# A seven-product down projection of 64-token blocks, with all token transposes between its first and second stretch

## The chip, the cores and the metric

One core of one Trainium2 chip runs the whole program. The metric is the device time of one execution in microseconds (us), median over the runs shown. TensorE (PE) multiplies, VectorE (DVE) and ScalarE (ACT) work element by element, GpSimd (POOL) issues the indirect transfers, SyncE (SP) issues the plain ones. Everything is float32.

## What is computed

A decoder block: a mixer (short convolution and a recurrent part), then a mixture of 32 experts of which each token takes 4, then a norm. The part that matters here is one expert's block of tokens:

```
h = xb @ gu_w[e] + gu_b[e]
x_glu = jnp.minimum(h[:, 0::2], SWIGLU_LIMIT)
x_lin = jnp.clip(h[:, 1::2], -SWIGLU_LIMIT, SWIGLU_LIMIT)
act = x_glu * jax.nn.sigmoid(SWIGLU_ALPHA * x_glu) * (x_lin + 1.0)
return act @ dn_w[e] + dn_b[e]
```

`gu_w[e]` is 1024 x 2048, `dn_w[e]` is 1024 x 1024. The result is scaled by the token's gate and added to the token's row of the output sum.

## The kernel before

The program first computes the mixer and the router (about a third of the time), and then goes through the 32 experts one after the other. An expert has room for 160 tokens: 128 in a full tile and 32 in "the rest". The rest's output is folded, four pieces of 32 tokens by 256 columns stacked on 128 partitions (`Y2`).

All engines run their own loop over the experts and meet at semaphores. TensorE's loop (`expert_pe`) is one turn behind itself: turn `n+1` first finishes expert `n` and then starts the next one. In a turn stand, in this order:

- `down_half(n, 0)`, L2083: 8 products of the activations (128 tokens as stationary operand, 128 rows of the feed-forward dimension each) with 512 columns of the down weights, into bank 2 of PSUM;
- `transpose_tokens`, L2102 and L2108: the gathered token rows of the expert after next (`xg`, and `xg2` for the rest) are transposed through the identity into banks 4, 5 and 7, from which ScalarE copies them into `xT` (`copy_xT`, L992 and L995);
- `down_rest(n)`, L2093, if the expert has more than 128 tokens: 32 products in tiles of 32 columns of the array, four side by side, into bank 6; otherwise one tiny product in its place (L2126);
- `down_half(n, 1)`, L2083 again: the other 512 columns, into bank 3;
- `gate_up`, L2063 (and its last 6 products, L2072): 128 products for the next expert, 16 for each of the 8 steps f, alternating between banks 0 and 1. The moving operand has 128, 144 or 160 tokens, by the size of the expert.

Every float32 product is two matmul records in the trace. VectorE follows with `glu`: for each f two additions and clips out of PSUM (L1468, L1469), then after ScalarE's sigmoid (L1000) two more operations (L1472, L1475) into `actT`. Step f of `gate_up` waits (`s_gd`) until the L1468 and L1469 of step f-2 have read their bank. At the end of the expert VectorE adds the bias to each finished bank (L1485 the first half, L1487 the rest, L1489 the second half), ScalarE scales by the gate (L1011, L1013, L1015), and GpSimd scatters the rows into the sum in memory (L703, L705). GpSimd's queue has, in this order: read the next list of tokens (L672, L673), gather those tokens (L687, L689), read the list for the scatter, scatter. The gather can start only when its list has landed, and that list is read behind the scatter of the expert before.

SyncE loads the weights: six slots of 2 MB, four for gate and up (`gu_w`), two for down (`dn_w`). The down slots of an expert are loaded when the down products of the expert before are done, that is when `gate_up` of the same expert starts.

Of the kernel before, what the change touches and what calls it, by code (L numbers as in the profile page):

```python
# [13 lines left out]
P = 128  # L14
# [101 lines left out]
def build(nc, x, xT_d, w_in_t, prm_d, lora_d, wgate_d, normw_d, w_out, router_w, router_b, gub_d, gu_w, dn_w,  # L116
          dn_b, consts_d, list0_d, entry_d, out, conv_d, bonus_d, xn_d, acc_d, list_d):
    ctx = ExitStack()
    with ctx:
# [121 lines left out]
        wslot = [at(o, KT, HALF) for o in (0, 16, 32, 64, 80, 96)]  # L241
        xg = at(48, D)
# [16 lines left out]
        sums = [at(112 + 8 * g, GROUP, D) if g < 3 else at(56, GROUP, D) for g in range(GROUPS)]  # L259
# [35 lines left out]
        s_ccp = sem("cc_copied")  # L295
        s_u = sem("u_made")
# [45 lines left out]
        s_wt = [sem(f"expert_w{u}") for u in range(6)]  # L342
# [4 lines left out]
        s_dn, s_db, s_yr, s_ye, s_l1 = sem("dn"), sem("dn_bias_in"), sem("y_rows"), sem("dn_read"), sem("lin")  # L347
        s_md = sem("experts_done")
# [51 lines left out]
        def weights_of(e, u):  # L400

            src = gu_w[bass.ds(4 * e + u, 1)] if u < 4 else dn_w[bass.ds(2 * e + u - 4, 1)]
            return src.rearrange("a p k n -> (a p) k n")
# [25 lines left out]
        def _(sp):  # L429
# [121 lines left out]
            for u in (2, 3, 4, 5):  # L551
                sp.dma_start(wslot[u], weights_of(0, u)).then_inc(s_wt[u], 16)

            def expert_weights(lo, r):
                with sp.Fori(lo, E) as e:
                    for u in range(6):

                        n = r * E + e
                        if u < 4:
                            sp.wait_ge(s_gu, 8 * n + 2 * u - 6)  # L560
                        else:
                            sp.wait_ge(s_dn, 3 * n)
                        sp.dma_start(wslot[u], weights_of(e, u)).then_inc(s_wt[u], 16)
                    sp.wait_ge(s_ye, 3 * n + 6)
                    bias_in(e)

            def sums_in():
                for g in range(GROUPS):
                    lo, hi = g * GROUP, (g + 1) * GROUP
                    sp.dma_start(sums[g], acc_d[lo * P:hi * P, :].rearrange("(t p) n -> p t n", p=P)).then_inc(s_x[g], 16)  # L570
# [4 lines left out]
            def experts_sp(r):  # L575
# [5 lines left out]
                sums_in()  # L581
# [21 lines left out]
        def _(pool):  # L603
# [6 lines left out]
            for ahead, by in ((s_ye, 6), (s_xe, 3), (s_gd, KT), (s_act, KT)):  # L610
                pool.sem_inc(ahead, by)
# [157 lines left out]
        def _(act):  # L769
# [232 lines left out]
            def expert_act(r):  # L1002
                copy_xT(r * (E + 1))
                with act.Fori(0, E - 1 if isinstance(r, int) else E) as e:
# [5 lines left out]
                    act.wait_ge(s_ye, 3 * n + 7)  # L1010
                    nc.scalar.activation(Yt[:, 0:HALF], Yt[:, 0:HALF], ACT.Copy, scale=gate).then_inc(s_yr, 1)  # L1011
                    act.wait_ge(s_ye, 3 * n + 8)
                    nc.scalar.activation(Y2, Y2, ACT.Copy, scale=gate2).then_inc(s_yr, 1)  # L1013
                    act.wait_ge(s_ye, 3 * n + 9)
                    nc.scalar.activation(Yt[:, HALF:D], Yt[:, HALF:D], ACT.Copy, scale=gate).then_inc(s_yr, 1)  # L1015
# [8 lines left out]
            def last_expert_act():  # L1024
# [14 lines left out]
                act.wait_ge(s_ye, 3 * n + 7)  # L1039
                nc.scalar.activation(sqj3[:, 0:HALF], rows[:, 0:HALF], ACT.Square, accum_out=rows_sq[:, 0:1]).then_inc(s_sq2, 1)  # L1040
                act.wait_ge(s_ye, 3 * n + 8)
                act.wait_ge(s_sq2, 2 * TT + 1)
                nc.scalar.activation(sqj3[:, 0:PW], rows2, ACT.Square, accum_out=rows_sq[:, 2:3]).then_inc(s_sq2, 1)
                act.wait_ge(s_ye, 3 * n + 9)
# [20 lines left out]
        def _(dve):  # L1065
# [202 lines left out]
            for h in range(2):  # L1268
                dve.wait_ge(s_ccp, h + 1)
                dve.wait_ge(s_pcv, 2 + h + 1)  # L1270
                nc.vector.tensor_tensor(u_cv[:, 2 + h * HALF:2 + (h + 1) * HALF], ccs[:, h * HALF:(h + 1) * HALF],
                                        ps[:, ring_pair(NR + 1) + h, :], ALU.mult).then_inc(s_u, 1)
            dve.wait_ge(s_u, 2)
# [202 lines left out]

            def expert_dve(r):
                with dve.Fori(0, E - 1 if isinstance(r, int) else E) as e:
                    n = r * E + e
                    for f in range(KT):  # L1480
                        glu(n, e, f)
                    dve.wait_ge(s_scr, n + 1)
                    dve.wait_ge(s_db, 16 * (PIECES + 1) * (n + 1))
                    dve.wait_ge(s_dn, 3 * n + 1)
                    nc.vector.tensor_tensor(Yt[:, 0:HALF], ps[:, 2, :], dnb[:, 0:HALF], ALU.add).then_inc(s_ye, 1)  # L1485
                    dve.wait_ge(s_dn, 3 * n + 2)
# [719 lines left out]
```

## Time and profile before

| | |
|---|---|
| runs shown | 2274.15, 2276.58, 2279.27 us; median 2276.58 us |
| profiled execution | 2280.95 us, of which the span from first to last instruction is 2279.3 us |
| TensorE busy | 2226.0 us, 98% of the span |
| VectorE, ScalarE, GpSimd busy | 781.6, 473.7, 343.5 us (34%, 21%, 15%) |
| DMA queues | 55.2% and 7.8% of 16 engines' span |
| mean granted clock of TensorE | 0.99 |

Busy shares are means over stages with different limits. A matmul record overlaps the next one, so the time that a product takes from TensorE is the distance between starts of records and not the duration of one.

### The profile page before, as it was taken

The numbers are of one execution on the slowest core, as the hardware profiler recorded it, in microseconds if no ns is written. First come the engines' busy times: TensorE is split into PE (matmuls) and PEld (weight loads), VectorE is DVE, ScalarE is ACT, GpSimd is POOL, SyncE is SP. The second block draws the span as 40 slices with busy tenths as digits, with TensorE's granted clock in tenths as the row PEclk, the third lists the DMA queues.
The fourth block names the chain that finished last, engine by engine and source line by source line (L and its number), as shares of the span: only waits on it lengthen the run. The fifth ranks groups of instructions, "written<-read, shape, count | busy, mean of one in ns | idle before, by whom it ended". The sixth has DMA issues, their size and how long they took to land.

```text
span 2279.3 us, 46156 instructions
## 1 busy us (share of the span) xinstructions
PE 2226.0 (98%) x18230; PEld 1644.5 (72%) x18231; DVE 781.6 (34%) x1853; ACT 473.7 (21%) x988; POOL 343.5 (15%) x360
## 2 busy tenths in 40 slices
PE   8999998899999999999999999999999999999997
PEld 3444445888445778887788878788778887788875
DVE  6465543455434222222222222232222232223224
ACT  3232001444333111111211111111111111111113
POOL 0000001121022212111121211122111121121112
PEclk9999999999998999999999999999999999999998
DMA  3111112334433767977777977789777988678877
GB/s 142 60 50 46 55 55 63 96 104 132 174 138 103 310 253 298 332 307 300 293 301 291 350 300 269 260 335 348 300 276 277 333 348 308 253 295 331 347 295 260
DMA packets 111411, 534.99 MB, mean 235 GB/s; under 512 B 26771, under 2 KB 60711, under 8 KB 86752
## 3 DMA queue, kind: packets, MB, share of 16 engines
q1 hardware_dynamic: 89200, 489.30, 55.2%
q0 software_dynamic: 22160, 44.98, 7.8%
q8 instruction: 36, 0.59, 0.1%
q14 instruction: 15, 0.12, 0.0%
HBM read 485.24 MB, written 40.05 MB: 230 GB/s over the span
## 4 chain that ended last, share of the span: by engine, by line
PE 95%; DMA 2%; DVE 1%; issue 1%; POOL 0%; ACT 0%; SPq 0%; POOLq 0%; DVEq 0%
PE ps L2063 39%; PE ps L2083 19%; PE ps L1571 9%; PE ps L1669 5%; PE ps L1942 5%; PE ps L2093 2%; PE ps L2072 2%; PE ps L1768 2%; PE ps L1618 1%; PE ps L1777 1%; PE ps L2102 1%; PE ps L1750 1%; DMA idx_g<-list_s 1%; PE ps L1782 1%; PE ps L1870 1%
## 5 line engine op out<-in xcount | busy, mean ns | idle before, releaser
L2063 PEld LDWEIGHTS ps<-arena 128*128 128x128 f32 x7808 | 925.9, 191 | 16.6 <-issue 15.1
L2063 PE MATMUL ps<-arena 128*128 128x128 f32 (+2 forms) x7808 | 926.9, 281 | 1.3 <-ACT arena L995 1.3
L2083 PE MATMUL ps<-arena 128*128 128x512 f32 x1024 | 454.3, 596 | 0.0
L2083 PEld LDWEIGHTS ps<-arena 128*128 128x128 f32 x1024 | 190.7, 190 | 221.8 <-issue 221.1
L1468 DVE TENSOR_SCALAR arena<-ps,arena 128x160 f32<-128x160 f32 x256 | 98.2, 384 | 620.1 <-PE ps L2063 536.1
L1000 ACT ACTIVATE arena<-arena 128x160 f32<-128x160 f32 x256 | 86.1, 336 | 828.3 <-DVE arena L1468 828.3
L1571 PE MATMUL ps<-arena 128*128 128x512 f32 x448 | 195.7, 594 | 0.0
L703 POOL DMA_INDIRECT sum_s<-arena,idx_s x31 | 51.5, 1663 | 824.6 <-ACT arena L1015 824.6
L1571 PEld LDWEIGHTS ps<-arena 128*128 128x128 f32 x448 | 84.5, 190 | 109.4 <-issue 109.4
L1669 PE MATMUL ps<-arena 128*128 128x512 f32 x280 | 120.6, 592 | 0.8 <-ACT arena L844 0.8
L1942 PE MATMUL ps<-arena 128*128 128x512 f32 x256 | 113.7, 594 | 0.0
L1669 PEld LDWEIGHTS ps<-arena 128*128 128x128 f32 x280 | 53.1, 190 | 68.1 <-issue 67.8
L1472 DVE SCALAR_TENSOR_TENSOR arena<-arena 128x160 f32<-128x160 f32 x256 | 83.3, 325 | 49.9 <-ACT arena L1000 48.9
L1469 DVE TENSOR_SCALAR arena<-ps,arena 128x160 f32<-128x160 f32 x256 | 95.9, 375 | 0.0
L687 POOL DMA_INDIRECT arena<-xn_s,idx_g x33 | 36.6, 1109 | 390.7 <-DMA idx_g<-list_s 361.4
L1489 DVE TENSOR_TENSOR arena<-ps,arena 128x512 f32<-128x512 f32 x31 | 21.4, 692 | 205.4 <-PE ps L2083 205.4
L1942 PEld LDWEIGHTS ps<-arena 128*128 128x128 f32 x256 | 47.6, 190 | 55.2 <-issue 54.9
L1475 DVE TENSOR_TENSOR arena<-arena 128x160 f32<-128x160 f32 x256 | 83.1, 325 | 8.8
L992 ACT COPY arena<-ps 128x512 f32<-128x512 f32 x66 | 35.4, 588 | 209.2 <-PE ps L2102 209.2
L1485 DVE TENSOR_TENSOR arena<-ps,arena 128x512 f32<-128x512 f32 x31 | 21.4, 691 | 158.6 <-PE ps L2083 158.6
L1015 ACT ACTIVATE arena<-arena,idx_s 128x512 f32<-128x512 f32 x31 | 22.4, 722 | 202.1 <-DVE arena L1489 202.1
L1768 PE MATMUL ps<-arena 64*64 64x64 f32 x1328 | 56.8, 224 | 6.2 <-issue 3.8
(271 smaller groups left out, 1965.5 us busy)
## 6 DMA issues: line engine op xcount, KB each, us to landing
arena<-gu_w SPq DMA_DIRECT2D x128, 2048.0 KB, 11.7
arena<-dn_w SPq DMA_DIRECT2D x64, 2048.0 KB, 14.6
arena<-dn_b SPq DMA_DIRECT2D x32, 512.0 KB, 16.2
arena<-w_in_t SPq DMA_DIRECT2D x26, 512.0 KB, 3.2
arena<-arena SPq DMA_DIRECT2D x50, 256.0 KB, 2.7
arena<-w_out SPq DMA_DIRECT2D x2, 2048.0 KB, 8.4
arena<-x SPq DMA_DIRECT2D x8, 512.0 KB, 5.2
xn_s<-arena SPq DMA_DIRECT2D x8, 512.0 KB, 2.7
```

The source lines that it names most:

```text
L703: pool.indirect_dma_start(acc_d, bass.IndirectOffsetOnAxis(ap=idx_s[:, 0:1], axis=0), Yt, None, compute_op=ALU.add).then_inc(s_sc, 16)
L1000: nc.scalar.activation(sgm[f % 2], gt[f % 2], ACT.Sigmoid, scale=ALPHA).then_inc(s_gs, 1)
L1468: nc.vector.tensor_scalar(gt[b], ps[:, b, 0:C], g0, LIMIT, ALU.add, ALU.min).then_inc(s_g1, 1)
L1469: nc.vector.tensor_scalar(lt[b], ps[:, b, C:2 * C], g1, LIMIT + 1, ALU.add, ALU.min).then_inc(s_gd, 1)
L1472: nc.vector.scalar_tensor_tensor(out=lt[b], in0=lt[b], scalar=1 - LIMIT, in1=sgm[b], op0=ALU.max, op1=ALU.mult).then_inc(s_l1, 1)
L1475: nc.vector.tensor_tensor(actT[:, f, :], lt[b], gt[b], ALU.mult).then_inc(s_act, 1)
L1571: last = nc.tensor.matmul(ps[:, bank + h, :], win[:, slot, kt * P:(kt + 1) * P], xnT[:, kt, h * HALF:(h + 1) * HALF], start=kt == 0, stop= ...
L1669: last = nc.tensor.matmul(ps[:, bank, :], weights[:, k * P:(k + 1) * P], tokens[:, k, :], start=start and k == 0, stop=stop and k == K2 - ...
L1768: last = nc.tensor.matmul(out_at(s, 0, h if l == 0 else 1 - h, r), MTs[s][own(h), r, :], Tst[s][own(h), r, :], start=True, stop=True)
L1942: last = nc.tensor.matmul(ps[:, 2 * (t % 2) + h, :], (mix_conv, mix_y)[part][:, k, t * P:(t + 1) * P], (woA, woB)[part][:, k, h * HALF:(h ...
L2063: last = nc.tensor.matmul(ps[:, f % 2, k * C:k * C + size], wslot[u][:, kt, o:o + P], xT[:, kt, 0:size], start=kt == 0, stop=kt == KT - 1, ...
L2083: last = nc.tensor.matmul(ps[:, 2 + h, :], actT[:, ft, 0:P], wslot[4 + h][:, ft, :], start=ft == 0, stop=ft == KT - 1)
```

## The change

The 128-token part of the down projection is split in four 64-token by 512-row blocks of activations and four 512-row by 512-column blocks of weights (d11, d12, d21, d22), and computed with seven products of blocks in place of eight, by sums and differences of blocks (Winograd's form of Strassen's scheme). One block product is 4 float32 matmuls with a stationary operand of 64 tokens. Two block products run side by side on the lower and upper 64 columns of the array (`both`). The seventh is cut in two halves of 256 columns that run side by side. The last expert keeps the old form, outside of the loop.

VectorE makes four sums of weight blocks (128 x 2048 elements each, in two pieces of 128 x 1024) between the `glu` steps, five small sums of activation blocks, and takes the results together in more and partly smaller steps than before. The down weights come in four transfers of 1 MB. The transposes stand between the first and the second stretch of products.

```diff
-            def down_rest(n):
+            def both(low, high, done):
+
+                for k in range(K2):
+                    for rows, (bank, acts, weights, first) in ((lower, low), (upper, high)):
+                        width = weights.shape[-1]
+                        last = nc.tensor.matmul(ps[rows, bank, 0:width], acts[:, k, :], weights[:, k, :],
+                                                start=first and k == 0, stop=k == K2 - 1, skip_group_check=True)
+                if done:
+                    last.then_inc(s_dn, 1)
+            def down_first(n, q, o):
+                pe.wait_ge(s_wd1, 32 * n + 32)
+                pe.wait_ge(s_as, 5 * q + 5 + 1)
+                pe.wait_ge(s_ds, 8 * q + 8 + 4)
+                pe.wait_ge(s_ye, o + 5)
+                both((2, a11, d11, True), (3, a_low, d12, True), True)
+            def down_second(n, q, o):
+                pe.wait_ge(s_as, 5 * q + 5 + 3)
+                pe.wait_ge(s_ds, 8 * q + 8 + 6)
+                pe.wait_ge(s_wd21, 16 * n + 16)
+                pe.wait_ge(s_ye, o + 6)
+                both((2, a_dif, d_mix, False), (2, a12, d21, True), True)
+            def down_third(n, m, q, o):
+                pe.wait_ge(s_ds, 8 * q + 8 + 8)
+                pe.wait_ge(s_xe, 3 * m + 4)
+                pe.wait_ge(s_ye, o + 7)
+                both((2, a_sum, d_dif, False), (4, a22, d_all, True), True)
+                pe.wait_ge(s_as, 5 * q + 5 + 5)
+                pe.wait_ge(s_ye, o + 8)
+                both((6, a_all, d22[:, :, 0:PW], True), (6, a_all, d22[:, :, PW:HALF], True), True)
...
                     with pe.If(turn > 0):
-                        down_half(n, 0)
+                        down_first(n, q, o)
                     size = size_at(turn)
-                    transpose_tokens(m)
+                    transpose_tokens(m, 0)
+                    transpose_tokens(m, 1)
+                    with pe.If(turn > 0):
+                        down_second(n, q, o)
                     with pe.If(size > 1):
-                        down_rest(n)
+                        down_rest(n, o, q)
...
                     with pe.If(turn > 0):
-                        down_half(n, 1)
+                        down_third(n, m, q, o)
```

```diff
+            def down_sums(n, q, f):
+                if f == 2:
+                    dve.wait_ge(s_wd1, 32 * n + 32)
+                    for h in range(2):
+                        down_sum(d_dif, d12, d11, ALU.subtract, h)
+                if f in (3, 4):
+                    dve.wait_ge(s_wd22, 16 * n + 16)
+                    down_sum(d12, d12, d22, ALU.subtract, f - 3)
+                if f in (4, 5):
+                    dve.wait_ge(s_ds, 8 * q + 8 + f - 3)
+                    down_sum(d_mix, d22, d_dif, ALU.subtract, f - 4)
+                if f == 6:
+                    dve.wait_ge(s_wd21, 16 * n + 16)
+                    for h in range(2):
+                        dve.wait_ge(s_ds, 8 * q + 8 + 5 + h)
+                        down_sum(d_all, d21, d_mix, ALU.subtract, h)
...
                     for f in range(KT):
                         glu(n, e, f)
+                        down_sums(n, q, f)
+                        if f == K2:
+                            dve.wait_ge(s_act, 8 * n + KT + K2)
+                            act_sum(q, a_low, a21, a11, ALU.subtract, 0)
+                    dve.wait_ge(s_act, 8 * n + KT + KT)
+                    act_sum(q, a_sum, a21, a22, ALU.add, 1)
+                    act_sum(q, a_dif, a_sum, a11, ALU.subtract, 2)
...
+                    dve.wait_ge(s_dn, o + 1)
+                    nc.vector.tensor_tensor(y_first[upper], ps[lower, 2, :], dnb[lower, 0:HALF], ALU.add).then_inc(s_ye, 1)
...
+                    dve.wait_ge(s_dn, o + 2)
+                    nc.vector.tensor_tensor(Yt[upper, 0:HALF], ps[lower, 2, :], dnb[lower, 0:HALF], ALU.add).then_inc(s_ye, 1)
+                    dve.wait_ge(s_ye, o + 7)
+                    nc.vector.tensor_tensor(Yt[lower, 0:HALF], y_first[upper], ps[upper, 2, :], ALU.add)
+                    nc.vector.tensor_tensor(Yt[upper, 0:HALF], Yt[upper, 0:HALF], ps[upper, 3, :], ALU.add).then_inc(s_yp, 1)
```

On TensorE, a turn of the loop in the kernel before stood so, from the first half of the down projection (bank 2) over the transposes and the rest (or the tiny product in its place) to the second half:

```order
L2083 MATMUL ps<-arena 128x512 [waits act_ready]
L2083 MATMUL ps<-arena 128x512 x6
...
L2102 MATMUL ps<-cst,arena 128x128 [waits tokens_gathered]
L2102 MATMUL ps<-cst,arena 128x128 x7
L2108 MATMUL ps<-cst,arena 128x128 [waits pieces_gathered]
...
L2093 MATMUL ps<-arena 32x256 [waits dn_read]
L2093 MATMUL ps<-arena 32x256 x31
...
L2083 MATMUL ps<-arena 128x512 [waits dn_read]
L2083 MATMUL ps<-arena 128x512 x7
```

In the changed kernel the same stretch stands so (L2199 is the line in `both`; 64 is the width of the stationary operand):

```order
L2199 MATMUL ps<-arena 64x512 [waits dn_read]
L2199 MATMUL ps<-arena 64x512 x7
...
L2234 MATMUL ps<-cst,arena 128x128 [waits tokens_gathered]
L2240 MATMUL ps<-cst,arena 128x128 [waits pieces_gathered]
...
L2199 MATMUL ps<-arena 64x512 [waits dn_read]
L2199 MATMUL ps<-arena 64x512 x7
...
L2182 MATMUL ps<-arena 32x256 [waits dn_read]
...
L2199 MATMUL ps<-arena 64x512 [waits dn_read]
L2199 MATMUL ps<-arena 64x512 x7
...
L2199 MATMUL ps<-arena 64x256 [waits dn_read]
L2199 MATMUL ps<-arena 64x256 x7
```

Two stretches of eight full-width products became three of eight half-width ones and one of eight that are half as wide and half as long; the transposes now come after the first of four stretches, and each stretch waits for a read by VectorE.

On VectorE, the end of an expert in the kernel before, from the last operation of the last `glu`:

```order
L1475 TENSOR_TENSOR arena<-arena 128x160 [waits lin]
L1482 REGISTER_ALU
L1483 REGISTER_ALU [waits expert_rows_free]
L1484 ISA [waits dn_bias_in]
L1485 TENSOR_TENSOR arena<-ps,arena 128x512 [waits dn]
L1486 REGISTER_ALU
L1487 TENSOR_TENSOR arena<-ps,arena 128x256 [waits dn]
L1488 REGISTER_ALU
L1489 TENSOR_TENSOR arena<-ps,arena 128x512 [waits dn]
```

And in the changed kernel, from the sums after the last `glu` to the last reads of PSUM:

```order
L1549 TENSOR_TENSOR arena<-ps,arena 64x512 [waits dn]
...
L1554 TENSOR_TENSOR arena<-ps,arena 64x512 [waits dn]
L1556 TENSOR_TENSOR arena<-arena,ps 64x512 [waits dn_read]
L1557 TENSOR_TENSOR arena<-arena,ps 64x512
...
L1559 TENSOR_TENSOR arena<-ps,arena 128x256 [waits dn]
...
L1561 TENSOR_TENSOR arena<-ps,arena 64x512 [waits dn]
L1562 TENSOR_TENSOR arena<-ps,arena 64x256
...
L1565 TENSOR_TENSOR arena<-arena,ps 64x512 [waits third_quarter_steps]
...
L1567 TENSOR_TENSOR arena<-arena,ps 64x512 [waits third_quarter_steps]
...
L1569 TENSOR_TENSOR arena<-arena,ps 64x256 [waits dn]
L1571 TENSOR_TENSOR arena<-arena,ps 64x256
```

Three reads of PSUM became eleven.

Two smaller parts: at the end of the program the sums are read back into the first two weight slots, and SyncE waits for the last expert's first steps before it issues those reads; and two semaphores of the convolution became one, whose first waiter now waits for both copies.

## Rows read from the trace of the kernel before

**Rows 1.** The page: the chain that ended last, share of the span by engine

```profile
PE 95%; DMA 2%; DVE 1%; issue 1%; POOL 0%; ACT 0%; SPq 0%; POOLq 0%; DVEq 0%
```

**Rows 2.** Timeline of TensorE, down part with rest: start us, us, engine, line, count

```profile
1974.88 7.03 PE L2083 MATMUL ps<-arena 128*128 128x512 f32 x16
1981.75 1.04 PE L2102 MATMUL ps<-cst,arena 128*128 128x128 f32 x8
1982.93 3.66 PE L2093 MATMUL ps<-arena 128*32 128x256 f32 x64
1986.52 7.13 PE L2083 MATMUL ps<-arena 128*128 128x512 f32 x16
1993.49 30.05 PE L2063 MATMUL ps<-arena 128*128 128x144 f32 x244
```

**Rows 3.** Timeline of TensorE, down part without rest

```profile
2072.51 7.03 PE L2083 MATMUL ps<-arena 128*128 128x512 f32 x16
2079.37 1.04 PE L2102 MATMUL ps<-cst,arena 128*128 128x128 f32 x8
2080.24 0.38 PE L2108 MATMUL ps<-cst,arena 128*128 128x128 f32 x2
2080.56 0.25 PE L2126 MATMUL ps<-cst,arena 128*32 128x32 f32 x2
2080.74 7.13 PE L2083 MATMUL ps<-arena 128*128 128x512 f32 x16
2087.71 27.41 PE L2063 MATMUL ps<-arena 128*128 128x128 f32 x244
```

**Rows 4.** Groups by line: all products of the rest

```profile
L2093 PE MATMUL ps<-arena 128*32 128x256 f32 x960 | 54.9, 380 | 0.0
```

**Rows 5.** Line L1875 in the recurrent part: durations ns, first and last start

```profile
L1875 PE MATMUL ps<-arena x16: 222/222/222, 411.1 to 411.5; 128*64 128x64 f32 x16
```

**Rows 6.** Timeline of VectorE in the turn of rows 3

```profile
2054.66 0.38 DVE L1468 TENSOR_SCALAR arena<-ps,arena 128x160 f32<-128x160 f32 x1 [2.04 <-PE ps L2063]
...
2068.95 0.38 DVE L1468 TENSOR_SCALAR arena<-ps,arena 128x160 f32<-128x160 f32 x1 [2.03 <-PE ps L2063]
...
2072.94 0.39 DVE L1468 TENSOR_SCALAR arena<-ps,arena 128x160 f32<-128x160 f32 x1 [2.45 <-PE ps L2072]
...
2074.16 0.33 DVE L1475 TENSOR_TENSOR arena<-arena 128x160 f32<-128x160 f32 x1
2079.57 0.69 DVE L1485 TENSOR_TENSOR arena<-ps,arena 128x512 f32<-128x512 f32 x1 [5.09 <-PE ps L2083]
```

**Rows 7.** Groups by line: VectorE on 1024 and on 256 elements

```profile
L1113 DVE TENSOR_TENSOR arena<-arena 128x1024 f32<-128x1024 f32 x14 | 17.1, 1224 | 44.9 <-ACT arena L791 44.9
L1487 DVE TENSOR_TENSOR arena<-ps,arena 128x256 f32<-128x256 f32 x31 | 13.2, 424 | 69.6 <-PE ps L2093 60.3 <-PE ps L2126 9.3
```

**Rows 8.** Down weights of one expert: SyncE's issue, and issue to landing

```profile
2088.05 0.89 SPq L563 DMA_DIRECT2D arena<-dn_w  x2
...
DMA to landing us min/median/max: 7.8/11.2/14.6
```

**Rows 9.** Timeline of GpSimd: the scatter behind the turn of rows 3

```profile
2090.22 1.67 POOL L703 DMA_INDIRECT sum_s<-arena,idx_s  x1 [23.20 <-ACT arena L1015]
```

**Rows 10.** DMA queues in 2051 to 2059.5 (two rows), then in 2072 to 2074.5 us

```profile
q1 hardware_dynamic: 215, 2.25, 64.9%
q0 software_dynamic: 210, 0.59, 35.9%
...
q0 software_dynamic: 55, 0.06, 6.6%
```

**Rows 11.** The chain that ended last, in order of time: the list behind the last scatter

```profile
2226.05 12.33 DMA idx_g<-list_s
```

**Rows 12.** Timeline of TensorE: the first time it reaches L2072

```profile
783.99 2.60 PE L2072 MATMUL ps<-arena 128*128 128x160 f32 x12 [2.94 <-issue]
```

**Rows 13.** Busy time by stretch: span, PE, PEld, DVE, ACT, POOL, clock, DMA share, GB/s

```profile
2043.60:2087.70 44.10, 44.10 (x301) 36.16 (x300) 12.41 (x35) 7.06 (x15) 8.10 (x8) 1.00 0.86 325
```

More of the change, by code:

```diff
@@ L241, in build @@
         wslot = [at(o, KT, HALF) for o in (0, 16, 32, 64, 80, 96)]
+        K2, TH = KT // 2, P // 2
+        d11, d21 = wslot[4][:, 0:K2, :], wslot[4][:, K2:KT, :]
+        d12, d22 = wslot[5][:, 0:K2, :], wslot[5][:, K2:KT, :]
+        d_dif, d_mix, d_all = (at(o, K2, HALF) for o in (112, 120, 128))
+        a_sum, a_dif, a_low, a_all = (at(56 + k, K2, TH) for k in range(4))
+        a_rest = at(60, K2, REST)
+        y_first, y_both = at(61, HALF), at(53, HALF)
         xg = at(48, D)
@@ L258, in build @@
         GROUPS = TT // GROUP
-        sums = [at(112 + 8 * g, GROUP, D) if g < 3 else at(56, GROUP, D) for g in range(GROUPS)]
+        sums = [at(8 * g, GROUP, D) for g in range(GROUPS)]
         rows, rows2 = at(178, D), at(182, PW)
@@ L341, in build @@
         s_mi = sem("moe_inputs")
-        s_wt = [sem(f"expert_w{u}") for u in range(6)]
+        s_wt = [sem(f"expert_w{u}") for u in range(4)]
+        s_wd1, s_wd22, s_wd21 = (sem(f"down_w{k}") for k in ("12_11", "22", "21"))
+        s_ds, s_as = sem("down_weight_sums"), sem("act_sums")
         s_ig, s_gx, s_is, s_sc = (sem("gather_list_in"), sem("tokens_gathered"), sem("scatter_list_in"),
@@ L609, in _ @@
                 pool.sem_inc(ahead, by)
-            for ahead, by in ((s_ye, 6), (s_xe, 3), (s_gd, KT), (s_act, KT)):
+            for ahead, by in ((s_ye, 5), (s_xe, 3), (s_gd, KT), (s_act, KT), (s_as, 5), (s_ds, 8)):
                 pool.sem_inc(ahead, by)
@@ L2076, in down_half @@
             def down_half(n, h):
-                pe.wait_ge(s_wt[4 + h], 16 * n + 16)
-                pe.wait_ge(s_ye, 3 * n + 4 + 2 * h)
+                pe.wait_ge(s_wd1, 32 * n + 32)
+                pe.wait_ge((s_wd21, s_wd22)[h], 16 * n + 16)
+                pe.wait_ge(s_ye, 5 * n + 5)
                 for ft in range(KT):
@@ L2085, in down_half, with down_rest @@
                 last.then_inc(s_dn, 1)
-            def down_rest(n):
-                pe.wait_ge(s_wt[5], 16 * n + 16)
-                pe.wait_ge(s_ye, 3 * n + 5)
+            def down_rest(n, o, q=None):
+                if q is not None:
+                    pe.wait_ge(s_as, 5 * q + 5 + 4)
+                pe.wait_ge(s_wd1, 32 * n + 32)
+                pe.wait_ge(s_wd22, 16 * n + 16)
+                pe.wait_ge(s_wd21, 16 * n + 16)
+                pe.wait_ge(s_ye, o + 5)
                 for ft in range(KT):
                     for g in range(PIECES):
-                        last = nc.tensor.matmul(ps[g * REST:(g + 1) * REST, 6, 0:PW], actT[:, ft, P:C],
+                        rows = a_rest[:, ft - K2, :] if q is not None and g >= 2 and ft >= K2 else actT[:, ft, P:C]
+                        last = nc.tensor.matmul(ps[g * REST:(g + 1) * REST, 6, 0:PW], rows,
                                                 wslot[4 + g // 2][:, ft, g % 2 * PW:(g % 2 + 1) * PW],
@@ L2096, in down_rest, with no_rest @@
                 last.then_inc(s_dn, 1)
-            def transpose_tokens(m):
-                pe.wait_ge(s_gx, 16 * m + 16)
-                for kt in range(KT):
+            def no_rest(o):
+                pe.wait_ge(s_ye, o + 5)
+                nc.tensor.matmul(ps[0:REST, 6, 0:REST], actT[:, 0, P:C], ident[:, 0:REST], start=True, stop=True
+                                 ).then_inc(s_dn, 1)
+            lower, upper = slice(0, TH), slice(TH, P)
+            def both(low, high, done):
[6 more added lines that the diff above has]
+                    last.then_inc(s_dn, 1)
@@ new lines, in down_third, with transpose_tokens @@
+            def down_third(n, m, q, o):
[6 more added lines that the diff above has]
+                both((6, a_all, d22[:, :, 0:PW], True), (6, a_all, d22[:, :, PW:HALF], True), True)
+            def transpose_tokens(m, part):
+                if part == 0:
+                    pe.wait_ge(s_gx, 16 * m + 16)
+                for kt in range(4 * part, 4 * part + 4):
@@ L2111, in expert_pe @@
+                if part == 1:
+                    pe.wait_ge(s_gx2, 16 * m + 16)
+                    for k in range(2):
+                        last = nc.tensor.transpose(ps[:, 7, k * P:(k + 1) * P], xg2[:, k * P:(k + 1) * P], ident)
+                    last.then_inc(s_xt, 1)
             def expert_pe(r):
@@ L2141, in expert_pe @@
                         gate_up_end()
+                if isinstance(r, int):
+                    n, m = E - 1, E
+                    size = size_at(E)
+                    down_half(n, 0)
+                    for part in range(2):
+                        transpose_tokens(m, part)
+                    with pe.If(size > 1):
+                        down_rest(n, 5 * n)
+                    with pe.If(size == 1):
+                        no_rest(5 * n)
+                    down_half(n, 1)
                 if isinstance(r, int):
```

125 lines of the change are left out of this document (78 added, 47 removed).

## The prediction

> **What bounds the kernel now.** I read the page first: the chain that ended last is TensorE for 95% [rows 1], so only what shortens TensorE's own stream counts, or a wait put into it. Then the timeline of TensorE for one turn of each kind. In the down part each row starts where the one before hands over, with no idle time noted: with a rest it goes from 1974.88 to 1993.49, 18.61 us [rows 2]; without one from 2072.51 to 2087.71, 15.20 us [rows 3]. The busy time by stretch says the same: TensorE 44.10 of 44.10 us, VectorE 12.41, transfers 86% [rows 13]. So there are two reserves, 31.7 us of VectorE and 14% of transfers per turn, and one bound. The change gives work from the bound to VectorE.
>
> How many turns of each kind: the rest's line has 960 records, 64 in a turn [rows 2, 4], so 15 experts have a rest. 31 experts are changed (the last one is not), so 16 changed ones have none.
>
> **The stream, term by term.** 16 records of 512 columns take 1981.75 - 1974.88 = 6.87 us, 0.429 each [rows 2]; a float32 product is two. A pair of 64-column stationaries that really run side by side should cost one such record per pass. Does the trace show that? L1875 is this shape with 64 columns of moving operand: 16 records start within 411.1 to 411.5 [rows 5], under 0.03 us each, while one full-width record of 64 columns would take 64/512 of 0.429 = 0.054. Side by side, then. The rest's four 32-wide tiles give the same for four different moving operands: 64 records in 3.59 us, 0.056 each [rows 2], where 256 columns alone would take 0.215. So:
>
> - three stretches of 8 pair steps: 24 x 0.429 = 10.30 us;
> - the seventh product: 8 pair steps of 256 columns, 0.215 each: 1.72 us;
> - transposes as now, 1.18 us; rest as now, 3.59 us, or the tiny product 0.18 [rows 2, 3].
>
> With rest 16.79 in place of 18.61, without 13.38 in place of 15.20: 1.82 us less in each of 31 turns, 56.4 us.
>
> **Changes of the array's shape.** Going from the transposes into a 32-wide tile costs more than a step: L2108 has two records, 0.11 each by the eight of L2102 in 0.87, but the next row starts 0.32 later, 0.10 too much [rows 3]. Coming back costs another 0.10: the second half takes 6.97 us, the first 6.87, for the same 16 records, and about 0.10 more stands before its start (0.18 for two records of 32 columns, 0.05 by their size) [rows 3]. A round trip is 0.3. A turn has one today, and two after the change: 31 x 0.3 = 9.3 us. Its bounds: nothing (if between 64 and 128 columns nothing is paid), and 0.6 a trip, 18.6 us, if going between 64 and 32 columns inside the second trip costs as much again.
> The Trainium skill, "TensorEngine Tiling (Array Packing)", Key Properties, says that a change of the tiling mode drains TensorE, which speaks against a form with more of them. The trace agrees that something is paid there, about 0.1 us at each change; if a drain meant waiting until a 512-column record is through (0.16 us beyond its step: 7.03 against 6.87 [rows 2]) at each of four changes, it would be 0.64 a turn and 20 us, not 9.3.
>
> **New waits of TensorE.** Times from 2072.51, the end of `gate_up`, in the turn of [rows 3], the tightest kind.
>
> - First stretch: its operands need only the sums after f = 4. No wait. It ends at 2075.94, the transposes at 2077.12 (0.1 later with the shape).
> - Second stretch: it needs `a_dif`, made after the last `glu`, and VectorE's read of the first. For this VectorE must be on time. A `glu` is 1.55 us (2072.94 to 2074.49) and comes every 3.57 us from 2054.66 (f = 2) to 2068.95 (f = 6) [rows 6]. A piece of a weight sum is 1.22 us [rows 7]; two are put after f = 2, 4 and 6, one after 3 and 5. Running this through: f = 3 starts 0.4 late, f = 5 about 0.85, f = 7 about 0.05; `gate_up` needs only the first two operations of f-2, over 2 us earlier, so no step of it waits. Then 2 x 0.42 for the activation sums [rows 7], ready near 2075.5. The read of the first stretch starts 0.20 behind its end (as L1485 behind L2102: 2079.57 to 2079.37) and takes 0.69 [rows 3, 6]: 2076.83. The transposes hide it until 2077.12, with 0.3 to spare. No wait; if that cover is gone it costs what is missing.
> - Third stretch: it needs VectorE's read of the second (L1554). With a rest, 3.59 us lie between: hidden. Without one only 0.18 lies between: 0.20 + 0.69, about 0.05 for the signal and 0.14 for the weight load make 1.08, less 0.18: 0.9 us, in 16 turns 14.4 us. The bounds are 0.7 and 1.2.
> - Seventh: needs L1559, in VectorE's queue 2.1 us of reads after L1554, and has 3.43 us of the third stretch over it. Hidden.
>
> Does any weight come late? The sums ask for the first two blocks after f = 2, at 2056.2, 12.6 us after `gate_up` began (the window of [rows 13] is this turn, from there to its end). The issue is 0.34 us after the beginning (2088.05 to 2087.71), and 2 MB land 7.8 us later, all 4 MB after 14.6 [rows 3, 8]; d22 is asked for after 16.6 and d21 after 27. Hidden by 4 us or more.
>
> **What is moved.** The transposes come 3.43 us earlier after `gate_up`, so the gather must be there earlier. In [rows 10] the last of it that carries data (55 packets, 0.06 MB) is moved in 2072 to 2074.5; its completion for the pieces, behind that, I put at 2076.2. The new L2108 would start at 2075.94 + 0.87 = 2076.8: 0.6 us to spare. Against that, the scatter ahead of it starts later: VectorE's queue after the third stretch has four reads (2.4 us) over a 1.72 us seventh product, then two of 0.42 [rows 6, 7], and then ScalarE scales both halves where today only one is left (I count 0.7 each, as VectorE's 0.69 for 512). The scatter is issued 3.4 us into `gate_up`, today 2.5 (2090.22 - 2087.71) [rows 3, 9]. 0.85 us later for scatter, list and gather would leave -0.25. For it speaks that the two queues alternate packet by packet (215 against 210) [rows 10], and that the down weights now come in 8 KB runs per partition in place of 16 KB, so the scatter's packets wait half as long each, 1 to 2.5 us in all. I take 0; the bounds are 0 and 1.4 us in 16 turns, 22 us. The end of the program hangs on this same chain (the list behind the last scatter, 12.33 us [rows 11]): -1 to +0.9 us, I take 0.9.
> New code is met cold once: the first L2072 waited 2.94 us [rows 12]. The loop's new stretch may do so once more, bounds 0 and 3: 1 us. The last expert's copy lies beside the sums' chain.
> The later sum reads and the joined semaphore cost nothing: the slots are free by f = 3, and the scatter lands later than that.
>
> **Sum.** -56.4 + 9.3 + 14.4 + 0.9 + 1.0 = -30.8 us. The profiled execution took 2280.95 (span 2279.3): 2250.1. The median of the runs is 4.4 lower: 2245.8, so 2246, 1.35% less.
>
> **Rivals.**
> 1. The waits are shorter or the changes of shape free: 56.4 - 11 (0.7 us x 16) - 2 = 43 saved, 2233. For it: [rows 5] show no loss inside a shape. Against: [rows 3] show 0.1 each. 0.15.
> 2. The gather is late in turns without a rest, or VectorE misses the 0.3 us: 1 to 1.4 us x 16, 16 to 22 us back, 2262 to 2268. For it: -0.25 if the packets change nothing. 0.20.
> 3. Slower than before, by VectorE's queue: the weight sums read and write 32 KB per partition beside transfers at 325 GB/s [rows 13]. Eight pieces lie before the last `glu`, with about 0.2 us of slack there and 1.6 in front of the second stretch. It decides when a piece takes 1.22 + (1.8 + 1.9)/8 = 1.7 us: then each of 16 turns waits 1.9 us more, and the 30.8 are gone; at 2 us per piece 2287. Against: 14 such pieces took 1224 ns on the mean [rows 7], though with fewer transfers beside them. 0.06.
> 4. The change doesn't do what it says: the pairs don't overlap at 512 columns. 31 x 12.0 = 373 us more, 2619. [rows 5] speak against. 0.02.
> 5. Nothing gained because transfers take over: a turn of 42.3 us needs 0.86 x 44.1 = 38 us of them [rows 13]. It would need 6 us more. 0.04, at 2272 to 2280.
>
> **How the numbers follow.** The forecast has 0.53, with its own range 2239 to 2255 from the bounds above. 2234 to 2266 leaves out half of rival 1, a part of 2, and 3 to 5: about 0.2. A difference under 0.2% (4.6 us) can't be told from none. Faster: 0.53 + 0.15 + 0.20, 0.88; within: most of rival 5, 0.04; slower: rivals 3, 4 and what I have not seen, 0.08.
>
> **What would show it.** In the trace after: L2199 in groups of 16 records with 64-column stationaries, 3.4 us a stretch and 1.7 for the seventh; `gate_up` as long as before (27.41 for 244 records of 128); down parts of about 14.6 and 17.1 us; an idle time of 0.9 us before the third stretch with L1554 as releaser in turns without a rest, and none before it elsewhere; VectorE busy near 29 us a turn (12.4 and 9.8 for the weight sums, 2.0 for the activation sums, 4.7 for more reads). Wrong if TensorE waits for the gather at L2240, for VectorE inside `gate_up` or before the second stretch, or if a pair step takes more than 0.43 us.

## The result, and the profile after

| | before | after |
|---|---|---|
| median of 4 runs each on one chip, us | 2276.18 | 2648.09 (2643.84 to 2666.75) |
| ratio, 95% interval | | 1.164, 1.158 to 1.170 |
| profiled execution, us | 2280.95 | 2666.75 |

The kernel became 372 us slower, where 30 us less was predicted. First the page of after: busy time by engine, and further down the shares of the chain that ended last.

```profile
PE 2304.3 (86%) x19222; PEld 1665.9 (63%) x19223; DVE 1259.8 (47%) x2504; ACT 478.4 (18%) x988; POOL 347.7 (13%) x360
...
PE 83%; issue 11%; DVE 4%; DMA 1%; ACT 1%; SPq 0%; DVEq 0%; POOL 0%; POOLq 0%; ACTq 0%
```

TensorE is still most of the chain, but no longer 95% of it [rows 1]: 11% is "issue", time in which an engine waited for nothing that the profile shows. Who stood still, and where, is in the waits of TensorE (us in total, times, longest):

```profile
PE ps L2146 <- issue: 178.8, 28, 10.6
PE ps L2155 <- issue: 51.1, 13, 4.2
PE ps L2199 <- DVE arena L1532: 47.2, 16, 3.4
PE ps L2199 <- issue: 26.9, 11, 4.1
PE ps L2199 <- DVE arena L1554: 9.7, 16, 0.6
```

Only the last line was predicted. L2146 is the first line of `gate_up`, L2155 its end, L2199 a pair of the new stretches. The first four lines make 304 us. The timeline of TensorE shows them in one turn without a rest, the kind of [rows 3]:

```profile
2021.85 1.79 PE L2155 MATMUL ps<-arena 128*128 128x160 f32 x12
2027.01 5.34 PE L2199 MATMUL ps<-arena 128*64 128x512 f32 x16 [3.36 <-DVE arena L1532]
2032.28 1.09 PE L2234 MATMUL ps<-cst,arena 128*128 128x128 f32 x8
2033.21 0.38 PE L2240 MATMUL ps<-cst,arena 128*128 128x128 f32 x2
2033.52 3.65 PE L2199 MATMUL ps<-arena 128*64 128x512 f32 x16
2037.10 0.25 PE L2189 MATMUL ps<-cst,arena 128*32 128x32 f32 x2
2037.96 5.38 PE L2199 MATMUL ps<-arena 128*64 128x512 f32 x32 [0.61 <-DVE arena L1554]
2052.77 29.87 PE L2146 MATMUL ps<-arena 128*128 128x128 f32 x244 [9.43 <-issue]
```

The second stretch is what the prediction said: 16 records in 3.65 us, so pairs run side by side at 512 columns. The third and the seventh product take 5.38, and before them stands the small wait on L1554. The rest was not foreseen: 9.43 us of nothing before `gate_up`, 3.36 before the first stretch. That one is put down to VectorE's L1532, so the timeline of VectorE is the check:

```profile
2025.01 0.33 DVE L1502 TENSOR_TENSOR arena<-arena 128x160 f32<-128x160 f32 x1
2025.37 0.89 DVE L1532 TENSOR_TENSOR arena<-arena 128x256 f32<-128x256 f32 x2
```

L1532 ended at 2026.26, TensorE began at 2027.01. The named engine was done 0.75 us before, where VectorE's reads follow TensorE's signal in 0.2 ([rows 3, 6]). Nor does the stretch need these sums: `down_first` waits only for the activation sum made after f = 4, and in `after_share16` below it starts at 2060.07, before the first L1532 of the same turn (2061.87). The profile names the semaphore that came last, not what held TensorE up. What did is among the queues (packets, MB, share of 16 engines). The page of before counts 36 packets of the queue that carries instructions, that of after:

```profile
q8 instruction: 281, 4.60, 0.8%
```

4.60 MB in 281 packets are 16 KB each. 245 more of them in 31 turns are 8 a turn. When they come says more. The same queue of after in 1000 to 2600 us, and in the gap of 9.43 us above (2043.3 to 2052.8):

```profile
q8 instruction: 228, 3.74, 1.1%
...
q8 instruction: 2, 0.03, 1.8%
```

In before the queue moves nothing at all between 1000 and 2270 us. So the loop's code is fetched again in turn after turn: 8 to 10 packets in most turns of after from the fourth on, 4 or 5 in two of them.

The gaps cost twice. The busy time by stretch gives, behind the times of the engines, the granted clock of TensorE (1.00 is 2.4 GHz), the share of the transfers and GB/s: first most of the loop, then 61 us from the end of the 9.43 us gap on, then the 3.5 us behind the gap of 3.36 and the 3.5 us after those.

```profile
747.60:2600.00 1852.40, 1544.42 (x11222) 1215.47 (x11220) 863.01 (x1736) 225.12 (x465) 255.35 (x250) 0.91 0.68 245
2052.80:2114.00 61.20, 47.21 (x333) 37.22 (x333) 27.76 (x56) 7.27 (x15) 8.11 (x8) 0.89 0.69 242
2027.00:2030.50 3.50, 3.49 (x10) 1.07 (x12) 0.00 (x0) 0.00 (x0) 0.00 (x0) 0.51 0.98 417
2030.50:2034.00 3.50, 3.50 (x23) 1.66 (x21) 1.31 (x3) 1.03 (x3) 0.00 (x0) 1.00 0.04 14
```

Behind these gaps TensorE goes on for some us at the lower of its two levels (1.2 GHz, 0.51 above): the first stretch takes 5.34 us, the same work without a gap ahead 3.65. `gate_up` takes 29.87 where 27.41 was its time [rows 3]. TensorE's busy time is 2304.3 us, 78 more than before, though its work fell: `after_share12` below, with the same stretches and no such gaps, has 2200.8, about 7 of them for products that it does wider. So about 110 us are the clock's (an estimate from these busy times). The 304 us of gaps, the 9.7 of the predicted wait and the 78 of busy time make 392; the span grew by 385.

### The profile page after: what moved, and what is told of

Read it like the earlier page. It is cut to its first block, busy times and chain, and to the rows that moved or that the text cites. A ratio compares the mean times of both kernels' runs of the same rounds, so it can differ in the third digit from the quotient of the medians.

```text
span 2664.6 us, 49505 instructions
## 1 busy us (share of the span) xinstructions
PE 2304.3 (86%) x19222; PEld 1665.9 (63%) x19223; DVE 1259.8 (47%) x2504; ACT 478.4 (18%) x988; POOL 347.7 (13%) x360
## 4 chain that ended last, share of the span: by engine, by line
PE 83%; issue 11%; DVE 4%; DMA 1%; ACT 1%; SPq 0%; DVEq 0%; POOL 0%; POOLq 0%; ACTq 0%
PE ps L2146 35%; PE ps L2199 16%; PE ps L1654 7%; PE ps L1752 5%; PE ps L2025 4%; PE ps L2182 2%; PE ps L2155 2%; PE ps L1851 2%; DVE arena L1508 1%; PE ps L2234 1%; PE ps L1701 1%; PE ps L1860 1%; PE ps L1833 1%; DVE arena L1532 1%; DVE arena L1495 1%
## 5 line engine op out<-in xcount | busy, mean ns | idle before, releaser
L2146 PE MATMUL ps<-arena 128*128 128x128 f32 (+2 forms) x7808 | 972.3, 289 | 179.6 <-issue 178.8
L2146 PEld LDWEIGHTS ps<-arena 128*128 128x128 f32 x7808 | 965.9, 199 | 193.5 <-issue 192.5
L2199 PE MATMUL ps<-arena 128*64 128x512 f32 x1984 | 436.1, 591 | 83.8 <-DVE arena L1532 47.2
L2199 PEld LDWEIGHTS ps<-arena 128*64 128x64 f32 x1984 | 145.2, 147 | 326.1 <-issue 301.2
L1508 DVE TENSOR_TENSOR arena<-arena 128x1024 f32<-128x1024 f32 x248 | 294.3, 1218 | 0.0
L1654 PE MATMUL ps<-arena 128*128 128x512 f32 x448 | 195.7, 594 | 0.0
L1654 PEld LDWEIGHTS ps<-arena 128*128 128x128 f32 x448 | 84.5, 190 | 109.4 <-issue 109.4
L2155 PE MATMUL ps<-arena 128*128 128x160 f32 x384 | 79.4, 372 | 51.1 <-issue 51.1
L1752 PE MATMUL ps<-arena 128*128 128x512 f32 x280 | 120.6, 592 | 0.8 <-ACT arena L871 0.8
L2025 PE MATMUL ps<-arena 128*128 128x512 f32 x256 | 113.7, 594 | 0.0
L2155 PEld LDWEIGHTS ps<-arena 128*128 128x128 f32 x384 | 72.4, 247 | 53.8 <-issue 53.8
L1752 PEld LDWEIGHTS ps<-arena 128*128 128x128 f32 x280 | 53.1, 190 | 68.1 <-issue 68.1
L1549 DVE TENSOR_TENSOR arena<-ps,arena 64x512 f32<-64x512 f32 x31 | 21.2, 684 | 150.4 <-PE ps L2199 150.4
L2025 PEld LDWEIGHTS ps<-arena 128*128 128x128 f32 x256 | 47.6, 190 | 55.2 <-issue 54.9
```

The costliest lines, as they stand in the source:

```text
L1508: nc.vector.tensor_tensor(dst[:, w, :], a[:, w, :], b[:, w, :], op).then_inc(s_ds, 1)
L1654: last = nc.tensor.matmul(ps[:, bank + h, :], win[:, slot, kt * P:(kt + 1) * P], xnT[:, kt, h * HALF:(h + 1) * HALF], start=kt == 0, stop= ...
L1752: last = nc.tensor.matmul(ps[:, bank, :], weights[:, k * P:(k + 1) * P], tokens[:, k, :], start=start and k == 0, stop=stop and k == K2 - ...
L2025: last = nc.tensor.matmul(ps[:, 2 * (t % 2) + h, :], (mix_conv, mix_y)[part][:, k, t * P:(t + 1) * P], (woA, woB)[part][:, k, h * HALF:(h ...
L2146: last = nc.tensor.matmul(ps[:, f % 2, k * C:k * C + size], wslot[u][:, kt, o:o + P], xT[:, kt, 0:size], start=kt == 0, stop=kt == KT - 1, ...
L2155: last = nc.tensor.matmul(ps[:, 1, C:2 * C], wslot[3][:, kt, 3 * P:4 * P], xT[:, kt, :], start=False, stop=kt == KT - 1, skip_group_check= ...
```

## The experiments

The question is what makes a loop's code be fetched again. A count of the built programs says how long the loop of experts is on TensorE: 1783 instructions before, 1859 after, at four instructions for each product (two weight loads, two matmuls). That is right for the float32 products and too much for the ten transposes of a turn. L2102 is eight transposes in each of 33 passes, and before has one weight load and one matmul for each:

```profile
L2102 PEld LDWEIGHTS ps<-cst,arena 128*128 128x128 f32 x264 | 30.9, 140 | 17.4 <-issue 17.4
L2102 PE MATMUL ps<-cst,arena 128*128 128x128 f32 x264 | 34.2, 273 | 0.0
```

So every length below, and in the expectations, is 20 too high, by the same amount in all kernels: steps and differences hold, the place of a limit shifts. Experiments go in both directions: shorten the loop of after, and lengthen that of before by code that is never run.

**A shorter loop, the same change.** `after_share16`. `SHARED` is how many products of `gate_up`'s last step stand once behind the branches on the block's size, not once in each of the three copies:

```diff
-        SHARED = 6
+        SHARED = 16
...
-                for f in range(KT):
+                for f in range(KT - 1):
...
-            def gate_up_end():
-                for kt in range(KT - SHARED, KT):
+            def gate_up_end(n):
+                pe.wait_ge(s_gd, 8 * n + KT + KT - 2)
+                for k in range(2):
+                    for kt in range(KT):
```

> The changed kernel with less code in TensorE's loop: the whole of step f = 7 (16 products, always 160 tokens wide) stands once behind the three branches, in place of 10 products in each branch and 6 behind them. The loop has 1777 instructions (4 per product) in place of 1859. Theory A (the code of the loop has outgrown what TensorE keeps, seven blocks of 256 instructions = 1792, and is fetched again in every turn): instruction packets fall from 281 to about 40, the idle time before gate_up goes, and the time is that of the prediction plus the wider step: 2246 + 12 (20 records by 0.025 us in 17 turns, by 0.013 in 12) = 2250 to 2265 us. Theory B (the idle time comes from the new waits on VectorE and the stretches themselves): all of it stays, 2640 to 2665 us.

Measured: 2270.72 us (2265.74 to 2280.56, 10 runs) against 2279.46; ratio 0.997, 0.9955 to 0.9985. The loop has 1777 instructions by this count, the new stretches are all in it, and 377 us are gone (the time is 5.7 us above the range expected for theory A, and 369 below that for B). The instruction packets are 32. So it isn't what the new stretches do; that it is how much code the loop holds, the next runs test. The timeline of TensorE, a turn without a rest:

```profile
2055.63 4.51 PE L2156 MATMUL ps<-arena 128*128 128x160 f32 x32
2060.07 3.65 PE L2200 MATMUL ps<-arena 128*64 128x512 f32 x16
2063.66 1.09 PE L2235 MATMUL ps<-cst,arena 128*128 128x128 f32 x8
2064.59 0.38 PE L2241 MATMUL ps<-cst,arena 128*128 128x128 f32 x2
2064.90 3.65 PE L2200 MATMUL ps<-arena 128*64 128x512 f32 x16
2068.49 0.25 PE L2190 MATMUL ps<-cst,arena 128*32 128x32 f32 x2
2069.34 5.38 PE L2200 MATMUL ps<-arena 128*64 128x512 f32 x32 [0.61 <-DVE arena L1554]
2074.65 5.51 PE L2146 MATMUL ps<-arena 128*128 128x128 f32 x47
```

No gap is left in this turn but the one predicted, and the down part takes 2074.65 - 2060.07 = 14.58 us.

**A longer loop, nothing else.** Code that is never reached is put at the end of the loop of before: one, four and twenty products (`before_dead1`, `before_dead4`, `before_dead20`); what is computed stays the same. The bound of the loaded size is raised so that the branch is not known to be dead:

```diff
-  size_i[0:1, bass.ds(r, 1), bass.ds(e, 1)], min_val=0, max_val=len(SIZES))
+  size_i[0:1, bass.ds(r, 1), bass.ds(e, 1)], min_val=0, max_val=9)
...
+                    with pe.If(need > 3):
+                        for kt in range(20):
+                            nc.tensor.matmul(ps[:, 0, 0:P], wslot[0][:, kt % KT, 0:P], xT[:, kt % KT, 0:P], start=True, stop=True)
```

> The kernel before with one product in a branch at the end of TensorE's loop that is never taken: the loop has 1789 instructions in place of 1783. Theory A (a limit of 1792): still inside, 2272 to 2282 us. Theory B (waits and stretches of the change): 2272 to 2282 us. Theory C (every added instruction costs, smoothly: 370 us for 76 instructions): about 2300 us.

> The same with four products that are never run: 1801 instructions, just over seven blocks of 256. Theory A: the loop no longer stays, instruction packets rise to 8 or 9 a turn, 2500 to 2680 us although no computation is added. Theory B: 2272 to 2282 us. Theory C: about 2360 us.

> The same with twenty products that are never run: 1865 instructions, about as many as the changed kernel's loop. Theory A: as with four, 2550 to 2700 us, and the excess over the kernel before is at least that of the changed kernel, whose own work is 31 us less: about 400 us. Theory B: 2272 to 2282 us. Theory C: about 2650 us.

Measured: one, 2279.59 (ratio 0.9989 to 1.0009); four, 2280.07 (0.9995 to 1.0014); twenty, 2646.32 (2586.20, 2638.76, 2653.88 and 2661.52) against 2279.46: 367 us more by the median, 307 by the lowest of four runs that scatter over 75. Theory A had expected an excess no less than that of the changed kernel (372 us), about 400; that part missed. The theory that had the limit at exactly seven blocks of 256 (1792) also expected four to be slow: it missed. But the miss is one of counting. Without the 20, four dead products make a loop of 1781, still under 1792, so this run does not speak against a limit there. Then three steps between, one run each (`before_dead8`, `before_dead12`, `before_dead16`):

> The kernel before with eight products that are never run, 1817 instructions in TensorE's loop; 1801 kept their place and 1865 did not. Theory A1 (the loop must end in the first part of the eighth block of 256, somewhere between slot 9 and 73 of it): either 2280 us with about 36 instruction packets or 2550 to 2660 with about 270, nothing between. Theory A2 (each further instruction costs some refetching): a time between, about 2370 us.

> The same with twelve, 1833 instructions. Theory A1: one of the two levels again, and the low one only if 1817 has it too. Theory A2: about 2460 us.

> The same with sixteen, 1849 instructions. Theory A1: one of the two levels, likely the high one, since the changed kernel has 1859. Theory A2: about 2550 us.

| kernel | loop as counted | without the 20 | us | instruction packets |
|---|---|---|---|---|
| before | 1783 | 1763 | 2279.46 | 36 |
| before_dead4 | 1801 | 1781 | 2280.07 | 36 |
| before_dead8 | 1817 | 1797 | 2278.63 | 36 |
| before_dead12 | 1833 | 1813 | 2611.73 | 256 |
| before_dead16 | 1849 | 1829 | 2616.47 | 256 |
| before_dead20 | 1865 | 1845 | 2646.32 (2586.20 to 2661.52) | 270 |

It is a step, not a slope: 16 instructions that are never run cost 333 us and 220 packets. Each side of the step has only one run, but twelve runs of before beside them lie between 2272.63 and 2281.26. The queue's line of `before_dead8`:

```profile
q8 instruction: 36, 0.59, 0.1%
```

and of `before_dead12`, and the first waits of its TensorE (L2083 is `down_half`, L2063 `gate_up`, L2072 its end):

```profile
q8 instruction: 256, 4.19, 0.7%
```

```profile
PE ps L2083 <- issue: 121.7, 24, 8.9
PE ps L2063 <- issue: 58.6, 25, 3.8
PE ps L2072 <- issue: 44.1, 11, 4.2
```

The timeline of the same kernel in one turn (not every turn is alike: the turn from 1463 to 1513 us has no gap and 3 packets):

```profile
2030.96 1.79 PE L2072 MATMUL ps<-arena 128*128 128x160 f32 x12
2036.93 10.16 PE L2083 MATMUL ps<-arena 128*128 128x512 f32 x16 [4.17 <-issue]
```

This is the signature of after in a kernel without any part of the change: a gap at the same place, before the first products of the down part, behind it 10.16 us for a half that took 7.03 [rows 2], and no VectorE to blame, since no semaphore came late.

**Long code, but not in the loop.** `before_dead20_behind`: the same twenty products, one level out, behind the loop.

> The kernel before with the same twenty products that are never run, behind TensorE's loop and not in it (loop 1783 instructions). Theory A (the loop's own length decides): 2274 to 2284 us and under 45 instruction packets. Theory D (the length of the whole program, or the copy of the last expert behind the loop, is what hurt the changed kernel): 2550 to 2650 us.

**What the sharing itself costs.** `before_share16` makes the edit of `after_share16` in the kernel before (loop 1701).

> The kernel before with all 16 products of f = 7 behind the branches (1701 instructions): what the wider step costs alone. From the rows of the changed kernel with the same edit (0.67 us a turn of 128 tokens, 0.46 one of 144) 11.4 + 5.5 = 17 us: 2290 to 2298 us. The seven products alone are then worth this less 2270.7: 20 to 27 us if the step by step sum holds (29 by its own turns, less the cold code).

Measured: 2290.23 (2288.18 to 2293.39); ratio 1.0053, 1.0040 to 1.0066. Work of the last step is done 160 columns wide for every expert, also where 128 would do; 12 us, where 17 had been reckoned, at the low end of the range. So the seven products alone, with the fetch out of the way, are worth 2290.23 - 2270.72 = 19.5 us by the medians, just under the 20 to 27 expected, and 24.5 by the two profiled spans (2291.7 and 2267.2). The first of these spans is of the slowest of five runs and the second of one faster than its median, so 24.5 is the more doubtful. Its timeline, for a comparison further down:

```profile
2078.60 4.51 PE L2073 MATMUL ps<-arena 128*128 128x160 f32 x32
2082.95 7.03 PE L2084 MATMUL ps<-arena 128*128 128x512 f32 x16
```

**As little sharing as fits.** `after_share14` (loop 1795) and `after_share12` (loop 1811):

```diff
-        SHARED = 6
+        SHARED = 12
...
-                        for kt in range(KT - SHARED if f == KT - 1 and k else KT):
+                        for kt in range(max(0, min(KT, (2 - k) * KT - SHARED)) if f == KT - 1 else KT):
```

> The changed kernel with 14 of the 16 products of step f = 7 behind the branches: 1795 instructions. With 16 shared it was 1777 instructions and 2270.7 us; two products less are 160 wide, 4 records by 0.027 in 17 turns and 0.013 in 12, 2.4 us less: 2266 to 2270 us if 1795 stays, as 1801 did in the kernel before. About 2640 if the limit for this loop is 1792.

> The changed kernel with 12 of the 16 products of step f = 7 behind the branches: 1811 instructions. 1817 kept its place in the kernel before, 1833 did not. If the limit is the same here: 2 us less than with 14, 2264 to 2268 us. If this loop's limit lies below 1811: about 2600.

Measured: 2267.90 (2265.17 to 2272.82), ratio 0.9964, 0.9952 to 0.9976; and 2265.91 (2264.14 to 2271.32), ratio 0.9953, 0.9940 to 0.9966. The second has the lowest time of this study, 12 us ahead of before and 382 ahead of after; its interval and that of `after_share14` overlap. In its timeline, a turn with a rest:

```profile
1961.15 3.65 PE L2200 MATMUL ps<-arena 128*64 128x512 f32 x16
1964.74 1.09 PE L2235 MATMUL ps<-cst,arena 128*128 128x128 f32 x8
1965.67 0.38 PE L2241 MATMUL ps<-cst,arena 128*128 128x128 f32 x2
1965.98 3.65 PE L2200 MATMUL ps<-arena 128*64 128x512 f32 x16
1969.57 3.66 PE L2183 MATMUL ps<-arena 128*32 128x256 f32 x64
1973.16 5.38 PE L2200 MATMUL ps<-arena 128*64 128x512 f32 x32
1978.47 21.70 PE L2146 MATMUL ps<-arena 128*128 128x144 f32 x175
```

18.61 us were the down part of such a turn [rows 2], now it is 1978.47 - 1961.15 = 17.32. Its waits of TensorE, in the loop, are the predicted one, and code met cold in the first turns:

```profile
PE ps L2200 <- DVE arena L1554: 9.7, 16, 0.6
...
PE ps L2156 <- issue: 3.6, 1, 3.6
...
PE ps L2146 <- issue: 1.2, 1, 1.2
```

**Where the transposes stand.** `after_share12_late` puts all token transposes behind the second stretch, as this diff shows:

```diff
-                    transpose_tokens(m, 0)
-                    transpose_tokens(m, 1)
                     with pe.If(turn > 0):
                         down_second(n, q, o)
+                    transpose_tokens(m, 0)
+                    transpose_tokens(m, 1)
```

> after_share12 with all transposes behind the second stretch in place of ahead of it. If the transposes hide VectorE's read of the first stretch as predicted: each of 31 turns now waits 0.85 us there (as the third stretch does in turns without a rest), and 16 turns lose their 0.67 us wait before the third: 26 - 11 = 15 us more than after_share12, about 2281 us. If the place of the transposes does not matter: the same as after_share12 within 3 us.

Measured: 2281.39 (2276.86 to 2288.82, 11 runs), 15.5 us more than `after_share12`, as expected; ratio to before 1.0015, 1.0005 to 1.0026. The waits, and the place in the timeline:

```profile
PE ps L2200 <- DVE arena L1549: 24.4, 31, 0.8
```

```profile
2026.76 3.65 PE L2200 MATMUL ps<-arena 128*64 128x512 f32 x16
2031.20 3.65 PE L2200 MATMUL ps<-arena 128*64 128x512 f32 x16 [0.79 <-DVE arena L1549]
```

Without cover, the second stretch waits 0.79 us in all 31 turns for VectorE's read of the first. The small wait on L1554 goes, since the transposes now hide that: 24.4 - 9.7 = 14.7 us of the 15.5. The transposes between the first and second stretch do hide this read, as the prediction had it, and save more there.

## Why the prediction was wrong

The step that failed is "New code is met cold once": the new code was priced as fetched once in the run, "bounds 0 and 3: 1 us". [rows 12] show one cold start of 2.94 us in 31 turns, and I read it as the nature of a loop; it was the state of a loop that still fits. I counted the matmuls of a turn and never the instructions of the loop with all its branches. The change made it 1859 long by the count above; between 1817 and 1833 the code stops staying, and the turns then pay 7 or 8 blocks of 16 KB on the mean. Measured: 304 us of gaps and about 110 of lower clock in place of 1 us. I had no rival for it. The cause is shown from both sides: the change without the length is fast (`after_share16`), the length without the change is slow (`before_dead12`).

The Trainium skill, "Runtime: NRT & Kernel Launch", section "Instruction fetch mechanics", gives TensorE room for 2048 instructions, refilled by blocks of 256, and says that a kernel need not fit, since the crossing is mostly hidden. It adds the warning that a taken branch to a target outside the current two blocks forces a fetch and a stall. The 16 KB packets agree with the blocks. The rest agrees in part: this loop with branches stays without any fetch at 1817 instructions as counted, far more than two blocks, and at 1833, still below 2048, fetches are not hidden but cost 333 us.

The other steps, read from `after_share12` and `after_share16`, where the fetch is gone:

| step | predicted, us | measured, us |
|---|---|---|
| the stream, pairs side by side | -56.4 | held: 3.65 for 16 records, last one's end included |
| changes of the array's shape | +9.3 (0 to 18.6) | about +22.3 |
| wait before the third stretch, 16 turns | +14.4 (11.2 to 19.2) | about +10.7 |
| second stretch, seventh product, `gate_up` | 0 | 0, no such wait |
| gather at its new place | 0 (0 to 22) | 0 to 0.4 |
| end of the program | +0.9 (-1 to +0.9) | +0.2 to +0.6 |
| code met cold | +1.0 (0 to 3) | +0.7 to +2, once |

- Changes of shape. A down part with a rest was to take 16.79 + 0.30 = 17.09 and takes 17.32. `gate_up` behind it takes 0.1 more: 25.28 for 224 records in `after_share16`, 25.17 in `before_share16`. The end of `gate_up` ahead of it takes 0.09 more: 2060.07 - 2055.63 = 4.44 there, 2082.95 - 2078.60 = 4.35 here. Together 0.72 a turn, not 0.30, and over my upper bound of 0.6. The estimate that took each of four changes at 0.16 (0.64 a turn) came nearest.
- The wait. From the end of the second stretch to the third there are 2069.34 - 2068.49 = 0.85 us, of which 0.18 is the tiny product: 0.67, where I had 0.9. The down part comes to 14.58, exactly what was predicted, by two errors of 0.23 that cancel.
- VectorE. I forecast 29 us a turn; the stretch of one turn in after shows 27.76. A turn of `after_share12` (2057.10 to 2101.04) has 27.83. It has room, and rival 3 did not happen. Nor did rival 4, though its 2619 us lies nearest to the result: the pairs overlap. A time that fits is no evidence for a mechanism.
- The sum without the fetch: -56.4 + 22.3 + 10.7 + 0.7 + 0.4 (the end of the program) = -22.3, between the 19.5 of the medians and the 24.5 of the spans. The forecast of -30.8 was 6 to 11 us too good, with 13 too little for the changes of shape, beside a missing term of 400.

## What to carry to other kernels

When a change adds instructions to a loop, count what the loop spans (on TensorE here; no other engine was tried), branches that are not taken included, and look how near it is to the length at which its code stops staying. The sign in a profile is the count of instruction packets: if it grows with the turns, time that is called "issue", or is put down to an engine that had long ended, is fetching. Copies of code in branches can be bought back by a few products that stand once behind them and are done a little wider; here that turned 372 us of loss into 12 of gain.

## What the hardware showed that I had not expected

- A loop on TensorE of up to 1817 instructions as counted (1797 without the 20 too many) is not fetched again: 32 to 37 packets of 16 KB in the whole run. From 1833 (1813) on there are 256 to 281, and the run is 333 to 372 us longer, 11 to 12 us for each of 31 turns. The bound between was not narrowed further, and whether the loop's place in the blocks of 256 moves it was not tried.
- How the cost goes on beyond the bound these runs can't tell: 334 us at 1833 and 339 at 1849 against the median of before beside them (2277.29), one run each, and 307 to 382 at 1865 in four runs.
- Code of the same size behind the loop costs nothing (ratio 1.0001).
- Behind a gap of 3 to 10 us TensorE runs at its lower level for a while: 5.34 for 3.65 us of work in after, 10.16 for 7.03 in `before_dead12`; granted 0.91 over the loop of after where it was 1.00. That adds about a third to the price of the gaps.
